# Second mixer's projections on unscaled rows, with the norm's factor applied behind each product

## The chip, the cores and the metric

The kernel is one program on one core of a Trainium2 chip. The metric is the device time of one execution in microseconds (us). The kernel before took 769.43 us (median of 3 runs, 769.27 to 769.75).

## The reference

Two transformer blocks run one after the other on 256 tokens of 1024 features, in float32.

```python
def reference(...):
    x = first_block(x, c, norm_mix_g, ...)      # adaLN, forgetting attention + pooling, 32-expert MoE, final rmsnorm
    return second_block(x, norm1_g_2, w_in_2, ...)

def hybrid_layer(x, ...):                        # the second block's mixer and feed-forward
    xn = rmsnorm_2(x, norm1_g[layer])
    u = xn @ w_in[layer]
    q_sb, k_sb, v_sb, f_raw, i_hg, q_hg, g_hg, gate_sb, gate_hg = jnp.split(u, list(c), axis=-1)
    o_sb = stick_breaking_attention(q_sb, k_sb, v_sb)
    f = lb + (1.0 - lb) * sigmoid(f_raw)
    o_hg = hgrn2_chunkwise(silu(q_hg), (1.0 - lb) * sigmoid(-f_raw), i_hg, log(f))
    o_hg = rmsnorm_2(o_hg, hg_norm_g) * silu(g_hg)
    g_a, g_b = sigmoid(gate_sb + bg[:D_MODEL]), sigmoid(gate_hg + bg[D_MODEL:])
    merged = g_a * (o_sb @ w_o_sb) + g_b * (o_hg @ w_o_hg)
    h = x + merged @ w_out
    a = square(relu(rmsnorm_2(h, norm2_g) @ w_ff1))
    return h + a @ w_ff2
```

The first block ends in an rmsnorm and the second begins with one. The kernel folds both into one factor for each token, which it calls `rq`. A factor for each token commutes with a product over the features, so it can be applied to the rows before `xn @ w_in` or to the result behind it.

## The kernel before

Every dense product is made of three passes of TensorE, because each operand is split in a high half and a low remainder of type fp32r: high times high, high times low, low times high (`mm3`). The weights come from HBM in pieces of 1 MB (128x2048 floats), loaded by SyncE (SP) into a ring of buffers in a fixed order. ScalarE (ACT) writes the high half of a piece (`whi`, L495, `act_pieces`), VectorE (DVE) then writes the remainder (`wlo`, L512, `dve_pieces`); a ring buffer is free for its next load when the remainder is written. There are four buffers of either half. The activations are split in the same way in `XH` and `XL`.

There is no planner: the order of work on each engine is written out by hand, one function for each engine, and semaphores join them. The pieces of the second mixer begin with piece 132 (`E1`): `f` uses pieces 132 and 133, `q2` 134 and 135, `g2` 136 and 137, `i2` 138 and 139, `sq` 140 and 141, `sk` 142 and 143, `sv` 144 and 145, then four pairs for the gates. `act_pieces(e, 137)` means: make high halves up to piece 136.

What stands around the change:

- The last expert group of the MoE (`pe_down`, `pe_combine`): the experts' results are made in two column halves n = 0 and 1. DVE scales a half to `ym` (L1331), TensorE adds it to the four accumulators of the residual rows (token half t, column half n).
- Then the norm. DVE multiplies the accumulators by a gain into `xn2` (`xg`, L1962). ACT and DVE sum squares (L1906, L1755, L2128), two tiny activations make `rq` (L1762, L1764), and DVE writes a diagonal matrix `hon` with `rq` on it (L1974, `factor`).
- Meanwhile TensorE runs four matmuls whose result nobody reads (`pe_awake`), then turns the 256 rows of 1024 features into 8 chunks of features by tokens (`n3`), by a matmul of `xn2` with `hon`, so that the turned rows come out scaled. ACT and DVE split each chunk (L1769, L1979), and between them the first pieces of weights. TensorE then computes `f`.
- DVE keeps the first block's output (`x_kept`, L1987), then prepares the lower bounds `lb` from a small table that SP loads after the MoE's end (L1989 to L2001). ACT takes the exponential of it (L1778) ahead of the high halves of pieces 134 to 136.
- Behind each product one engine reads the PSUM bank: DVE for `f` (L2006), ACT for `q2`, `g2` (silu, L1912), `sq`, `sk` (L737, L1819), `i2`, `sv` (L742) and the 16 gate chunks with their bias (`act_gate`, L1941).
- GpSimd (POOL) makes decay exponents for the four recurrent heads, ACT takes their exponential (`act_decays`), DVE multiplies (`dve_decays`), TensorE makes scores (`pe_head`) between the projections.
- The eight heads of the stick-breaking attention follow in a software pipeline over i = 1 to 10: scores `z`, softplus on ACT and DVE, weights `w`, their exponential on ACT (`w_exp`, L1839), product with the values (`sbv`). The last gate projections and the output projection of the recurrent heads (`o_hg`) stand between them. `act_sigmoids` at i = 2 and i = 5 loads the sigmoid's table, runs one activation over eight gate chunks (L1949) and loads the former table again.

SP has a queue of its own for loads, and POOL does no step that is moved here.

## Time and profile before

| | |
|---|---|
| median of 3 runs | 769.43 us |
| span of the profiled execution, first to last instruction | 767.3 us |
| what lies around the span (769.43 - 767.3) | 2.1 us |
| TensorE busy | 689.3 us, 90% |
| VectorE, ScalarE, GpSimd busy | 47%, 38%, 6% |
| end of the MoE to the start of the second mixer's products | 350 to 365 us of the span |
| second mixer | 365 to 583 us, then the feed-forward |

All times of places in the text are us from the start of the span. The profile names an instruction by its line, engine and operation, with the tile that it writes and what it reads. "PE" is TensorE's matmuls, "PEld" its weight loads. An fp32 matmul is recorded as two instructions. A bracket behind a row says how long the engine had been idle before it and what ended that. "PEclk" is the clock granted to TensorE, as a share of full speed.

### The profile page before, as it was taken

The numbers are of one execution on the slowest core, as the hardware profiler recorded it, in microseconds if no ns is written. First come the engines' busy times: TensorE is split into PE (matmuls) and PEld (weight loads), VectorE is DVE, ScalarE is ACT, GpSimd is POOL, SyncE is SP. The second block draws the span as 40 slices with busy tenths as digits, with TensorE's granted clock in tenths as the row PEclk, the third lists the DMA queues.
The fourth block names the chain that finished last, engine by engine and source line by source line (L and its number), as shares of the span: only waits on it lengthen the run. The fifth ranks groups of instructions, "written<-read, shape, count | busy, mean of one in ns | idle before, by whom it ended". The sixth has DMA issues, their size and how long they took to land.

```text
span 767.3 us, 13033 instructions
## 1 busy us (share of the span) xinstructions
PE 689.3 (90%) x5466; PEld 536.6 (70%) x5466; DVE 357.3 (47%) x569; ACT 295.3 (38%) x432; POOL 46.5 (6%) x84
## 2 busy tenths in 40 slices
PE   3999999899758677778999999999999999999996
PEld 2987778743323222223999989998979999999995
DVE  3568861521110000105846786536576744555443
ACT  4244530331111010005764553678355643354432
POOL 0000000000000000000074650000000000000000
PEclk9999999999988888879999999999999999999999
DMA  8999899999999999999855334414345445654001
GB/s 355 403 416 402 323 424 419 422 423 422 423 423 422 423 421 425 396 414 422 305 204 218 114 114 167 161 34 187 111 164 193 150 179 220 220 209 170 6 1 55
DMA packets 33038, 210.27 MB, mean 274 GB/s; under 512 B 4688, under 2 KB 5072, under 8 KB 8656
## 3 DMA queue, kind: packets, MB, share of 16 engines
q1 hardware_dynamic: 32976, 209.38, 68.4%
q8 instruction: 46, 0.75, 0.4%
q14 instruction: 16, 0.13, 0.0%
HBM read 208.32 MB, written 1.05 MB: 273 GB/s over the span
## 4 chain that ended last, share of the span: by engine, by line
PE 69%; DMA 20%; DVE 5%; ACT 3%; issue 2%; SPq 2%; DVEq 0%; ACTq 0%
PE psum L419 67%; DMA raw<-in_w_exp 16%; DMA raw<-in_w_in_t 3%; SPq L474 1%; PE psum L427 1%; DVE wlo L512 1%; ACT whi L495 1%; DMA raw<-in_w_ada_q 1%; DVE XL L1979 0%; DVE X L2428 0%; DVE acc L534 0%; ACT G L1283 0%; ACT XT L2375 0%; ACT Sp L838 0%; DVE ym L1331 0%
## 5 line engine op out<-in xcount | busy, mean ns | idle before, releaser
L419 PE MATMUL psum<-XH,whi 128*128 128x256 f32 x736 | 210.1, 286 | 4.3 <-DVE XL L665 3.2
L419 PE MATMUL psum<-XH,wlo 128*128 128x256 f32 x736 | 208.1, 283 | 0.0
L419 PE MATMUL psum<-XL,whi 128*128 128x256 f32 x736 | 207.9, 282 | 0.0
L512 DVE TENSOR_TENSOR wlo<-raw,whi 128x2048 fp32r<-128x2048 f32 (+1 forms) x88 | 169.0, 1958 | 48.9 <-ACT whi L495 48.9
L495 ACT ACTIVATE whi<-raw 128x2048 fp32r<-128x2048 f32 (+1 forms) x79 | 139.4, 1801 | 39.8 <-PE psum L419 22.4
L419 PEld LDWEIGHTS psum<-XH,whi 128*128 128x128 f32 x736 | 139.1, 189 | 7.9 <-DVE XL L665 3.6
L419 PEld LDWEIGHTS psum<-XL,whi 128*128 128x128 f32 x736 | 138.6, 188 | 0.3
L419 PEld LDWEIGHTS psum<-XH,wlo 128*128 128x128 f32 x736 | 138.8, 189 | 0.0
L419 PE MATMUL psum<-raw,G 128*32 128x512 f32 x456 | 69.3, 698 | 18.7 <-DMA raw<-in_w_exp 18.1
L419 PEld LDWEIGHTS psum<-raw,G 128*32 128x32 f32 x456 | 18.1, 125 | 57.1 <-issue 56.4
L419 PE MATMUL psum<-raw,XT 128*32 128x512 f32 x248 | 37.9, 747 | 19.3 <-DMA raw<-in_w_exp 18.1
L1267 ACT ACTIVATE WT<-psum 128x256 f32<-128x256 f32 x8 | 3.1, 384 | 134.7 <-PE psum L419 98.7
L419 PE MATMUL psum<-whi,FL 128*128 128x512 f32 (+1 forms) x132 | 50.6, 384 | 0.0
L419 PE MATMUL psum<-wlo,FH 128*128 128x512 f32 (+1 forms) x132 | 50.6, 384 | 0.0
L419 PE MATMUL psum<-whi,FH 128*128 128x512 f32 (+1 forms) x132 | 50.5, 383 | 0.0
L419 PEld LDWEIGHTS psum<-raw,XT 128*32 128x32 f32 x248 | 10.3, 132 | 42.1 <-issue 42.1
L1331 DVE TENSOR_TENSOR ym<-psum,GT 128x512 f32<-128x512 f32 x16 | 11.1, 691 | 58.7 <-PE psum L419 58.7
L1321 DVE TENSOR_TENSOR XT<-XT,psum 128x256 f32<-128x256 f32 x8 | 3.4, 421 | 67.0 <-ACT XT L1272 67.0
L1733 POOL TENSOR_TENSOR XT<-xn 128x128 f32<-128x128 f32 x12 | 9.3, 777 | 401.5 <-DVE xn L2018 388.2
L419 PE MATMUL psum<-ym,WT 128*128 128x512 f32 x64 | 29.1, 595 | 1.8 <-DVE ym L1331 1.8
L2395 DVE TENSOR_TENSOR af<-af,psum 128x512 f32<-128x512 f32 x16 | 11.0, 687 | 39.1 <-ACT af L2354 39.1
L2354 ACT ACTIVATE af<-psum 128x512 f32<-128x512 f32 x16 | 9.6, 599 | 50.4 <-PE psum L419 50.4
(347 smaller groups left out, 943.7 us busy)
## 6 DMA issues: line engine op xcount, KB each, us to landing
raw<-in_w_exp SPq DMA_DIRECT2D x85, 1024.0 KB, 22.7
raw<-in_w_ff SPq DMA_DIRECT2D x32, 1024.0 KB, 5.9
raw<-in_w_in SPq DMA_DIRECT2D x22, 1024.0 KB, 6.3
raw<-in_w_ada SPq DMA_DIRECT2D x16, 1024.0 KB, 11.7
raw<-in_w_in_t SPq DMA_DIRECT2D x8, 1024.0 KB, 18.0
X<-in_w_exp SPq DMA_DIRECT2D x5, 1024.0 KB, 24.8
raw<-in_w_ada_q SPq DMA_DIRECT2D x4, 1024.0 KB, 17.2
raw<-in_w_out_t SPq DMA_DIRECT2D x4, 1024.0 KB, 9.8
```

Source lines behind the costliest of these rows:

```text
L419: return e.matmul(o, l, r, start=start, stop=stop, skip_group_check=True)
L427: return e.transpose(o, x, C["ident"][0:p, 0:p])
L474: e.dma_start(dst, src).then_inc(small[name], 16)
L495: e.activation(whi[j % NS][:, x], ring[slot[i]][:, x], ACT.Copy).then_inc(*hi_made(("hi", j), ("hi", j, x.start // 1024)))
L512: e.tensor_tensor(wlo[j % NS][:, x], ring[slot[i]][:, x], whi[j % NS][:, x], ALU.subtract).then_inc(*steps_(("lo", j, x.start // 1024), *[ ...
L1267: e.activation(WT[y % 2][:, :], bank(("w", y))[:, 0:256], ACT.Copy).then_inc(*moe_act(("read", ("w", y)), ("WT", y)))
L1321: e.tensor_tensor(ac[b], sa[b], bank(("gu", y))[:, 256:512], ALU.mult).then_inc(*moe_dve(("read", ("gu", y)), ("act", y)))
L1331: e.tensor_tensor(ym[:, y % 2, cs], bank(("d", y, n))[:, :], GTF[:, cs], ALU.mult).then_inc(*moe_dve(("read", ("d", y, n)), ("y", y, n)))
L1733: e.tensor_tensor(ev[:, :, 1, :], bv[:, :, 1, :], ref, ALU.subtract).then_inc(*hyb_pool())
L2354: e.activation(af[q][:, :], bank((("ff1", j), q))[:, :], ACT.Relu).then_inc(*ff_act(("relu", j, q)))
L2395: e.tensor_tensor(af[q][:, :], af[q][:, :], bank((("ff1", j), q))[:, :], ALU.mult).then_inc(*ff_dve(("read", (("ff1", j), q)), ("square", ...
```

## The change

The turned rows are no longer scaled: `pe_n3` turns `xn2` by transposes against the identity. The first two groups of chunks (features 0 to 511) are turned between the experts' last `pe_down` and the last `pe_combine`, the other two between parts of `f`. The four `pe_awake` matmuls go. `rq` is computed later, and a new matmul with ones makes `rq` as a row in every partition (`rq_row`), which DVE copies to `RQ`. Every feature-major product is then multiplied by `RQ` by DVE as it leaves PSUM (`dve_scaled`, `dve_gate`), so ACT's readers of `sq`, `sk` and the gates go, and silu works on the scaled copy. The token-major products `i2` and `sv` take `rq` as ACT's scale. The gates' bias moves into the sigmoid, which becomes eight activations of one chunk in place of one over eight.

```diff
@@ -1505,6 +1506,9 @@
                     for n in range(2):
                         pe_down(e, db, y - 1, n)
                         if y == NQ:
+                            if n:
+                                pe_n3(e, Banks([1]), 0)
+                                pe_n3(e, Banks([3]), 1)
                             pe_combine(e, y - 1, n)
...
@@ -1750,27 +1754,24 @@
...
-            for t in range(2):
-                e.wait_ge(*at(("xg", t, 0)))
-                e.activation(flat(gates[:, 0:4, :])[:, 512 * t:512 * t + 512], xn2[:, t, 0:512], ACT.Square,
-                             accum_out=sq2[:, t:t + 1]).then_inc(*hyb_act(("sq2", t)))
-            high_part(e, E1, 0)
-            for t in range(2):
-                e.wait_ge(*at(("xg", t, 1)))
-                act_square(e, t, 1)
+            for q in range(4):
+                if q == 2:
+                    for t in range(2):
+                        act_square(e, t, 1)
+                high_part(e, E1 + q // 2, q % 2)
+                e.wait_ge(*at(("n3", "turned", q)))
+                for c in (2 * q, 2 * q + 1):
+                    e.activation(XH[:, c, :], bank(("n3", q))[:, 256 * (c % 2):256 * (c % 2) + 256], ACT.Copy,
+                                 scale=gcol[:, 2, c:c + 1]).then_inc(*hyb_act(("n3", "H", c)))
+            cur["act"] = E1 + 2
+            for t in range(2):
+                e.activation(flat(gates[:, 4 * t:4 * t + 4, :]), xn2[:, t, :], ACT.Square, accum_out=sq2[:, t:t + 1]).then_inc(
+                    *hyb_act(("sq2", t)))
...
-            high_part(e, E1, 1)
-            for q in range(4):
-                e.wait_ge(*at(("n3", "turned", q)))
-                for c in (2 * q, 2 * q + 1):
-                    e.activation(XH[:, c, :], bank(("n3", q))[:, 256 * (c % 2):256 * (c % 2) + 256], ACT.Copy,
-                                 scale=gcol[:, 2, c:c + 1]).then_inc(*hyb_act(("n3", "H", c)))
-                if q < 2:
-                    high_part(e, E1 + 1, q)
-            cur["act"] = E1 + 2
+            e.wait_ge(*at("s1"))
...
@@ -1798,30 +1799,23 @@
                 e.activation(hgb[:, h, :], tmpB[:, o:o + 256], ACT.Ln, bias=lb[:, h:h + 1], scale=oml[:, h:h + 1]).then_inc(
                     *hyb_act(("f_log", h)))
             e.preload_act_table(ACT.Silu)
+            act_pieces(e, 140)
             act_silu(e, hgq, "q2")
-            act_pieces(e, 140)
+            act_pieces(e, 142)
             act_silu(e, hgg, "g2")
             e.preload_act_table_set("natural_log_exp_and_others")
-            act_pieces(e, 142)
             act_decays(e, 0)
             for t in range(2):
-                act_rows(e, hgv, t, hyb_act, "i2")
+                act_rows(e, hgv, t, hyb_act, "i2", rq[:, t:t + 1])
             act_pieces(e, 144)
             for hd in range(4):
                 if hd == 0:
-                    act_copy(e, sbq, 0.125, hyb_act, "sq")
                     act_pieces(e, 146)
                 if hd < 3:
                     act_decays(e, hd + 1)
                 for q in range(2):
-                    if hd == 0:
-                        e.wait_ge(*at(("sk", "mm", q)))
-                        e.activation(flat(sbk[:, 2 * q:2 * q + 2, :]), bank(("sk", q))[:, :], ACT.Copy).then_inc(
-                            *hyb_act(("read", ("sk", q)), ("sk", "out", q)))
-                    elif hd == 1:
-                        act_rows(e, sbv, q, hyb_act, "sv")
-                    else:
-                        act_gate(e, 4 * (hd - 2), q)
+                    if hd == 1:
+                        act_rows(e, sbv, q, hyb_act, "sv", rq[:, q:q + 1])
                     if q == 0:
                         act_head(e, hd)
...
@@ -1838,8 +1832,6 @@
                         e.wait_ge(*at(("sbv", h - 2)))
                     e.activation(zs[h % 2], bank(("z", h))[:, 0:384], ACT.Exp).then_inc(*hyb_act(("read", ("z", h)), ("w_exp", h)))
                 act_pieces(e, SB_PIECES[i])
-                if 1 <= i <= 4:
-                    act_gate(e, 8 if i < 3 else 12, (i - 1) % 2)
...
         def act_square(e, t, n):
-            e.wait_ge(*at(("combined", NQ - 1, n, t)))
+            e.wait_ge(*at(("xg", t, n)))
             e.activation(flat((hgq, hgg)[t][:, 2 * n:2 * n + 2, :]), ps[4 + 2 * t + n][:, :], ACT.Square,
-                         accum_out=(ss, ss2)[n][:, t:t + 1]).then_inc(*hyb_act(("sq", t, n)))
+                         accum_out=(ss, ss2)[n][:, t:t + 1]).then_inc(*hyb_act(("sq", t, n), *[("read", ("acc", t))] if n else []))
 
         def act_silu(e, dst, name):
             for q in range(2):
-                e.wait_ge(*at((name, "mm", q)))
-                e.activation(flat(dst[:, 2 * q:2 * q + 2, :]), bank((name, q))[:, :], ACT.Silu).then_inc(
-                    *hyb_act(("read", (name, q)), (name, "out", q)))
+                e.wait_ge(*at((name, "scaled", q)))
+                e.activation(flat(dst[:, 2 * q:2 * q + 2, :]), flat(dst[:, 2 * q:2 * q + 2, :]), ACT.Silu).then_inc(
+                    *hyb_act((name, "out", q)))
...
-        def act_gate(e, base, q):
...
-                e.activation(gates[:, base + n, :], bank(("gate", base, q))[:, o:o + 256], ACT.Identity,
-                             bias=nbg[:, base + n:base + n + 1]).then_inc(
-                    *hyb_act(*[("read", ("gate", base, q))] if n % 2 else []))
-
         def act_sigmoids(e, o):
             e.preload_act_table(ACT.Sigmoid)
-            e.wait_ge(*hyb_act.last())
-            g = flat(gates[:, o:o + 8, :])
-            e.activation(g, g, ACT.Sigmoid).then_inc(*hyb_act(("sig", o)))
+            e.wait_ge(*loaded("bg"))
+            for n in range(o, o + 8):
+                e.wait_ge(*at(("gate", 4 * (n // 4), n % 4 // 2)))
+                e.activation(gates[:, n, :], gates[:, n, :], ACT.Sigmoid, bias=nbg[:, n:n + 1]).then_inc(*hyb_act(("sig", o)))
             e.preload_act_table_set("natural_log_exp_and_others")
...
         def dve_hybrid(e):
             e.wait_ge(*loaded("fin"))
-            for t, n in ((0, 0), (1, 0), (0, 1), (1, 1)):
-                cs = slice(512 * n, 512 * n + 512)
-                if t < n:
-                    dve_results(e, NQ - 1, (1,))
-                e.wait_ge(*at(("combined", NQ - 1, n, t) if n else ("sq", t, n)))
-                e.tensor_tensor(xn2[:, t, cs], ps[4 + 2 * t + n][:, :], GTM[:, cs], ALU.mult).then_inc(*hyb_dve(("xg", t, n)))
-            dve_second_sum(e, 0)
+            for t in range(2):
+                dve_xg(e, t, 0)
+            dve_results(e, NQ - 1, (1,))
+            low_part(e, E1, lo_dve, 0)
+            dve_n3(e, 0)
+            for t in range(2):
+                dve_xg(e, t, 1)
+            low_part(e, E1, lo_dve, 1)
+            dve_n3(e, 1)
+            dve_n3(e, 2)
+            low_part(e, E1 + 1, lo_dve, 0)
+            dve_n3(e, 3)
+            low_part(e, E1 + 1, lo_dve, 1)
+            cur["dve"] = E1 + 2
             e.wait_ge(*at(("sq", 1, 1)))
-            e.tensor_tensor(ss[:, :], ss[:, :], ss2[:, :], ALU.add).then_inc(*hyb_dve("s1", ("read", ("acc", 0)), ("read", ("acc", 1))))
-            dve_second_sum(e, 1)
-            e.wait_ge(*at("s1"))
+            e.tensor_tensor(ss[:, :], ss[:, :], ss2[:, :], ALU.add).then_inc(*hyb_dve("s1"))
+            e.wait_ge(*hyb_dve.last())
+            e.wait_ge(*at(("sq2", 1)))
             e.scalar_tensor_tensor(out=sq2[:, :], in0=ss[:, :], scalar=1e-6, in1=sq2[:, :], op0=ALU.mult, op1=ALU.add).then_inc(*hyb_dve())
             e.wait_ge(*hyb_dve.last())
-            e.scalar_tensor_tensor(out=rq[:, :], in0=sq2[:, :], scalar=D * 1e-12, in1=sq3[:, :], op0=ALU.add, op1=ALU.add).then_inc(
-                *hyb_dve("u"))
+            e.tensor_scalar(rq[:, :], sq2[:, :], D * 1e-12, None, ALU.add).then_inc(*hyb_dve("u"))
             e.wait_ge(*at("rq"))
             for t in range(2):
                 e.tensor_scalar(hon[:, t, :], C["ident"], rq[:, t:t + 1], None, ALU.mult).then_inc(*hyb_dve(("factor", t)))
-            low_part(e, E1, lo_dve, 0)
-            for q in range(4):
-                for c in (2 * q, 2 * q + 1):
-                    e.wait_ge(*at(("n3", "H", 2 * q + 1)))
-                    e.scalar_tensor_tensor(out=XL[:, c, :], in0=bank(("n3", q))[:, 256 * (c % 2):256 * (c % 2) + 256],
-                                           scalar=gcol[:, 2, c:c + 1], in1=XH[:, c, :], op0=ALU.mult, op1=ALU.subtract).then_inc(
-                        *hyb_dve(*[("n3", "ready", q), ("read", ("n3", q))] if c % 2 else []))
-                if q < 3:
-                    low_part(e, E1 + (q + 1) // 2, lo_dve, (q + 1) % 2)
-            cur["dve"] = E1 + 2
...
+            e.wait_ge(*at("rq_row"))
+            e.tensor_copy(RQ, bank("rq_row")[:, 0:256]).then_inc(*hyb_dve(("read", "rq_row")))
+            e.wait_ge(*hyb_dve.last())
             for q in range(2):
-                e.wait_ge(*at(("f", "mm", q)))
-                e.tensor_scalar(tmpA[:, 512 * q:512 * q + 512], bank(("f", q))[:, :], -1.0, 87.0, ALU.mult, ALU.min).then_inc(
-                    *hyb_dve(("read", ("f", q)), ("f_neg", q)))
+                dve_scaled(e, tmpA.rearrange("p (a b) -> p a b", a=4), q, "f", -1.0)
+                e.wait_ge(*hyb_dve.last())
+                e.tensor_scalar(tmpA[:, 512 * q:512 * q + 512], tmpA[:, 512 * q:512 * q + 512], 87.0, None, ALU.min).then_inc(
+                    *hyb_dve(("f_neg", q)))
...
+            dve_pieces(e, 140)
+            for q in range(2):
+                dve_scaled(e, hgq, q, "q2")
             dve_pieces(e, 142)
+            for q in range(2):
+                dve_scaled(e, hgg, q, "g2")
             dve_decays(e, 0)
             dve_pieces(e, 144)
             for hd in range(4):
                 if hd == 0:
+                    for q in range(2):
+                        dve_scaled(e, sbq, q, "sq", 0.125)
                     dve_head(e, 0)
                     dve_pieces(e, 146)
                 if hd < 3:
                     dve_decays(e, hd + 1)
+                if hd == 0:
+                    dve_scaled(e, sbk, 0, "sk")
+                if hd >= 2:
+                    dve_gate(e, 4 * (hd - 2), 0)
...
+                if hd == 0:
+                    dve_scaled(e, sbk, 1, "sk")
+                if hd == 2:
+                    dve_gate(e, 0, 1)
...
                 dve_pieces(e, 148 + 2 * hd)
+                if hd == 3:
+                    dve_gate(e, 4, 1)
...
+                if i <= 4:
+                    dve_gate(e, 8 if i < 3 else 12, (i - 1) % 2)
...
-        def dve_second_sum(e, t):
-            e.wait_ge(*at(("xg", t, 1)))
-            e.scalar_tensor_tensor(out=flat(gates[:, 4:8, :])[:, 512 * t:512 * t + 512], in0=xn2[:, t, 512:1024], scalar=1.0,
...
+        def dve_xg(e, t, n):
+            cs = slice(512 * n, 512 * n + 512)
+            e.wait_ge(*at(("combined", NQ - 1, n, t)))
+            e.tensor_tensor(xn2[:, t, cs], ps[4 + 2 * t + n][:, :], GTM[:, cs], ALU.mult).then_inc(*hyb_dve(("xg", t, n)))
...
+        def dve_scaled(e, dst, q, name, by=None):
+
+            d, p = dst[:, 2 * q:2 * q + 2, :], bank((name, q))[:, :].rearrange("p (a b) -> p a b", a=2)
+            e.wait_ge(*at((name, "mm", q)))
+            if by is None:
+                i = e.tensor_tensor(d, p, row2(RQ), ALU.mult)
+            else:
+                i = e.scalar_tensor_tensor(out=d, in0=p, scalar=by, in1=row2(RQ), op0=ALU.mult, op1=ALU.mult)
+            i.then_inc(*hyb_dve(("read", (name, q)), (name, "scaled", q)))
+
+        def dve_gate(e, base, q):
+            if base == 8:
+                e.wait_ge(*at(("hm_last", 3)))
+            e.wait_ge(*at(("gate", base, "mm", q)))
+            e.tensor_tensor(gates[:, base + 2 * q:base + 2 * q + 2, :], bank(("gate", base, q))[:, :].rearrange("p (a b) -> p a b", a=2),
+                            row2(RQ), ALU.mult).then_inc(*hyb_dve(("read", ("gate", base, q)), ("gate", base, q)))
...
-            pe_awake(e, 4, ("gu", NQ - 1))
-            for q in range(4):
-                p = banks.take(e, ("n3", q))
-                for c in (2 * q, 2 * q + 1):
-                    for t in range(2):
-                        e.wait_ge(*at(("factor", t)))
-                        i = mm(e, p[:, 256 * (c % 2) + 128 * t:256 * (c % 2) + 128 * t + 128], xn2[:, t, 128 * c:128 * c + 128],
-                               hon[:, t, :], c % 2 + t == 0, True)
-                i.then_inc(*hyb_pe(("n3", "turned", q)))
-            for q in range(4):
-                feature_part(e, banks, w2(q // 2), (2 * q, 2 * q + 1), "f", "n3", hyb_pe)
+            fb = Banks([0, 2])
+            feature_part(e, fb, w2(0), (0, 1), "f", "n3", hyb_pe)
+            pe_n3(e, Banks([4]), 2)
+            pe_n3(e, Banks([5]), 3)
+            feature_part(e, fb, w2(0), (2, 3), "f", "n3", hyb_pe)
+            feature_part(e, fb, w2(1), (4, 5), "f", "n3", hyb_pe)
+            p = Banks([3]).take(e, "rq_row")
+            for t in range(2):
+                e.wait_ge(*at(("factor", t)))
+                i = mm(e, p[:, 128 * t:128 * t + 128], C["ones"], hon[:, t, :], t == 0, True)
+            i.then_inc(*hyb_pe("rq_row"))
+            feature_part(e, fb, w2(1), (6, 7), "f", "n3", hyb_pe)
...
+        def pe_n3(e, banks, q):
+            p = banks.take(e, ("n3", q))
+            for t in range(2):
+                e.wait_ge(*at(("xg", t, q // 2)))
+                for c in (2 * q, 2 * q + 1):
+                    i = turn(e, p[:, 256 * (c % 2) + 128 * t:256 * (c % 2) + 128 * t + 128], xn2[:, t, 128 * c:128 * c + 128])
+            i.then_inc(*hyb_pe(("n3", "turned", q)))
```

## Rows read from the trace of the kernel before

**Rows 1.** Page: busy time by engine, and the chain that ended last by engine

```profile
PE 689.3 (90%) x5466; PEld 536.6 (70%) x5466; DVE 357.3 (47%) x569; ACT 295.3 (38%) x432; POOL 46.5 (6%) x84
PE 69%; DMA 20%; DVE 5%; ACT 3%; issue 2%; SPq 2%; DVEq 0%; ACTq 0%
```

**Rows 2.** Chain of waits in order of time, 355 to 577 (start, us, what)

```profile
355.50 5.39 PE psum L419 x12
...
371.33 1.91 ACT whi L495
...
373.34 1.76 DVE wlo L512
...
375.55 2.30 DVE wlo L512
...
575.58 0.87 PE psum L427 x8
```

**Rows 3.** Timeline of TensorE, 355 to 378 (start, us, engine, line, operation, tiles, count, idle before)

```profile
355.50 1.96 PE L419 MATMUL psum<-ym,WT 128*128 128x512 f32 x4 [0.91 <-DVE ym L1331]
360.92 3.81 PE L419 MATMUL psum<-hon,xn 128*128 128x128 f32 x32
364.48 0.37 PE L419 MATMUL psum<-XH,whi 128*128 128x256 f32 x1
...
377.98 0.36 PE L419 MATMUL psum<-XH,whi 128*128 128x256 f32 x1 [0.43 <-DVE wlo L512]
```

**Rows 4.** Timeline of ACT and DVE, 352 to 379

```profile
354.67 0.69 DVE L1331 TENSOR_TENSOR ym<-psum,GT 128x512 f32<-128x512 f32 x1 [0.47 <-PE psum L419]
363.75 1.21 DVE L512 TENSOR_TENSOR wlo<-raw,whi 128x1024 fp32r<-128x1024 f32 x1
370.83 0.15 DVE L1989 TENSOR_TENSOR lb<-lbr 128x4 f32<-128x4 f32 x1
371.22 0.20 ACT L1778 ACTIVATE lb<-lb 128x4 f32<-128x4 f32 x1 [3.79 <-DVE lb L1991]
377.75 1.28 DVE L2006 TENSOR_SCALAR xn<-psum 128x512 f32<-128x512 f32 x2
```

**Rows 5.** SP's issue at 357 to 359, and that load's time to landing (last column)

```profile
357.75 0.33 SPq L474 DMA_DIRECT2D lbr<-in_lb_cols  x1
lbr<-in_lb_cols SPq DMA_DIRECT2D x1, 4.0 KB, 11.8
```

**Rows 6.** Timeline of ACT, DVE and PE, 519 to 535

```profile
519.98 0.84 ACT L1941 ACTIVATE gates<-psum,nbg 128x256 f32<-128x256 f32 x2 [2.08 <-PE psum L419]
520.71 1.05 ACT L1847 ACTIVATE XH<-hgg 128x1024 fp32r<-128x1024 f32 x1
523.80 3.70 ACT L495 ACTIVATE whi<-raw 128x2048 fp32r<-128x2048 f32 x2
528.82 1.92 ACT L1949 ACTIVATE gates<-gates 128x2048 f32<-128x2048 f32 x1
534.13 0.85 PE L419 MATMUL psum<-sbv,xn 128*128 128x64 f32 x6 [1.31 <-issue]
```

**Rows 7.** ACT by line: duration ns min/median/max, first and last start, forms

```profile
L1941 ACT ACTIVATE gates<-psum,nbg x16: 467/471/477, 462.2 to 520.3; 128x256 f32<-128x256 f32 x16
L1798 ACT ACTIVATE hgb<-xn,lb,oml x4: 583/588/590, 383.5 to 385.0; 128x256 f32<-128x256 f32 x4
```

**Rows 8.** TensorE's two idle stretches nearest in length (timeline), and the clock behind one (stretch, us, PE busy, PEclk, DMA)

```profile
18.46 0.39 PE L419 MATMUL psum<-XH,whi 128*128 128x256 f32 x1 [2.38 <-DVE XL L665]
201.07 5.34 PE L419 MATMUL psum<-raw,G 128*32 128x512 f32 x32 [3.36 <-DMA raw<-in_w_exp]
201.50:204.25 2.75, 2.75 (x17) 0.50 1.01 429
```

**Rows 9.** The core from 378 to 486: us, busy of PE, PEld, DVE, ACT, POOL, PEclk, DMA, GB/s

```profile
378.00:486.00 108.00, 108.00 (x1200) 99.66 (x1201) 73.19 (x125) 59.16 (x79) 46.36 (x80) 1.00 0.47 174
```

**Rows 10.** Timeline of DVE, 435 to 439, ahead of the second head's scores

```profile
438.91 0.49 DVE L2147 TENSOR_TENSOR xn<-psum,cst 128x320 f32<-128x320 f32 x1 [2.82 <-PE psum L419]
```

More of the change, by code:

```diff
@@ L738, in act_copy, with act_rows @@
                     *steps_(("read", (name, q)), (name, "out", q)))
-        def act_rows(e, dst, t, steps_, name):
+        def act_rows(e, dst, t, steps_, name, scale=1.0):
             e.wait_ge(*at((name, "mm", t)))
-            e.activation(dst[:, t, :], bank((name, t))[:, :], ACT.Copy).then_inc(*steps_(("read", (name, t)), (name, "out", t)))
+            e.activation(dst[:, t, :], bank((name, t))[:, :], ACT.Copy, scale=scale).then_inc(*steps_(("read", (name, t)), (name, "out", t)))
         def sp_mixer(e):
@@ L2277, in pe_z @@
                 for q in range(2):
-                    e.wait_ge(*at(("sq", "out", q)))
-                    e.wait_ge(*at(("sk", "out", q)))
+                    e.wait_ge(*at(("sq", "scaled", q)))
+                    e.wait_ge(*at(("sk", "scaled", q)))
             mm(e, p[:, 0:256], sbk[r, h // 2, 0:128], sbq[r, h // 2, 0:256], True, False)
@@ L2488, in tensor_engine @@
             pe_moe(e, Banks(list(range(8))))
-            banks = Banks(list(range(8)))
+            banks = Banks([6, 7, 0, 1, 2, 3, 4, 5])
             pe_hybrid(e, banks)
```

16 lines of the change are left out of this document (7 added, 9 removed).

## The prediction, on record before the changed kernel ran

> **What bounds the kernel now.** I read the page first. TensorE is busy 90% of the span and the chain that ended last is 69% TensorE [rows 1], so only time in which TensorE waits, or does work that can go, is worth anything. The chain in order of time shows where that is: beside the MoE's loads, which the change leaves alone, it leaves TensorE around the end of the MoE and is back on it at 378 [rows 2]. The timeline of TensorE there has three things to see [rows 3]: the last combine at 355.50, then matmuls that only keep the engine busy, then the scaled turning at 360.92 (32 records, 3.81 us) and `f` at 364.48. One wait follows, 0.43 us at 377.98 for a weight remainder. Behind it TensorE is busy for all of the next 108 us [rows 9], so whatever is saved must be saved before 378 and kept.
>
> **What sets 377.98.** This is the step on which the forecast rests. `q2` needs the remainders of pieces 134 and 135. DVE makes them at 373.34 and 375.55, behind ACT's high half of 134 at 371.33 [rows 2]. ACT could start that only behind its tiny exponential of `lb` (371.22), which waits for DVE's two `lb` steps from 370.83 [rows 4]. From the first `lb` step to the high half is 0.50 us, from the high half to TensorE's restart 6.65 us. So `f` may begin much earlier and still gain only what this ACT and DVE chain gains.
>
> **The front, step by step.** Removed on TensorE: four matmuls that nobody reads (in the 5.39 us of [rows 2]) and 16 scaling matmuls, 3.81 us. Added: 16 transposes; eight of the same kind took 0.87 us for the feed-forward's norm [rows 2]. Eight of them fall between the last `pe_down` and the combine, where TensorE idles 0.91 us for DVE's `ym` [rows 3]: they fit, and I take them as free. DVE's `xg` of the first half no longer waits for ACT's square, so ACT's square, high half and first split of `XH` follow from about 352.7. By the durations of the rows (half of 1.91 for half a high piece [rows 2], 1.21 for half a remainder, 0.69 for a PSUM product of 512 [rows 4]) the first `XL` is ready at 357.4, right behind the combine's end (355.50 + 1.96). `f` starts at 357.5 instead of 364.48. Its 96 matmuls took from 364.48 to about 375.8, 11.4 us; with 0.9 us of turning and about 1.0 us of waiting for and making `rq_row` in between it ends at 370.8.
>
> ACT and DVE meanwhile alternate through the eight chunk splits and four half pieces, ACT squares 2 x 1024 columns for `rq` (about 1.2 us each), and DVE has `factor` at 367.3 and `x_kept` at 368.6. That is 2.2 us ahead of 370.83. But `lb` reads a table that SP issues at 357.75, when the MoE has ended, and which lands 11.8 us later, at 369.55 [rows 5]; it stands behind the pieces in the queue, and nothing here moves it. Before, that load was hidden by 1.3 us; now it is what comes last. `lb` starts at 369.6, the high half of 134 at 370.1, and TensorE gets the remainder of 135 at 370.1 + 6.65 = 376.75: **a gain of 1.2 us**, against 7 us for the start of `f`.
>
> **What the gap does to TensorE.** Between `f`'s end at 370.8 and the first remainder (370.1 + 375.55 - 371.33 = 374.3) TensorE is now idle 3.5 us. The trace of before has an idle stretch of 2.38 us behind which TensorE kept its clock (18.46), and one of 3.36 us behind which it ran at the granted clock 0.50, which is 1.2 GHz, through 204.25 at least [rows 8]. I take the nearer row: the clock falls. The 12 matmuls that need piece 134 alone (1.4 us at full clock) then take 2.8, from 374.4 to 377.2, of which 0.45 lies behind piece 135; if the low stretch is as long as that row's, 3.2 us, its last 0.4 loses 0.2 more. Together 0.7 us, bounds 0 (no fall) and 1.6 (3.2 us halved with no cover). Front in all: -1.2 + 0.7 = **-0.5 us**. The Trainium skill speaks against the change here: "TensorE: Matmul & The Clock Gate", section "What's actually happening", says that throttled is the default state and activity releases it, and its Part 4 that transposes do not count as activity in the same way. By that rule the fall is likely and the front gives 0.5; without it the front would give 1.2. The row at 201.07 agrees for an idle engine, and no row here tests transposes.
>
> **DVE's new work.** Sixteen products of 512 columns from PSUM at 0.69 [rows 4], 11 us in all, move to DVE or are new; `f` needs a second instruction of about 0.4 for each half and DVE copies `RQ` (0.4). Queued behind a product that waits for its projection are DVE's next remainders, decays and heads. For `f` this adds 1.5 us on DVE behind 376.7, so the scan and POOL's decays come about 0.3 us later than before; their users are 10 us away. The tightest place is the second head: the product of `sk`'s second half ends 0.7 us behind `sk`'s end, and DVE was idle 2.82 us before it read the scores at 438.91 [rows 10]. It fits. At the end of the recurrent heads ACT's gate copy goes (0.84 less before two high halves) and a DVE product comes (0.69): -0.1. I take all others at 0; if one has no cover it costs its 0.69, bounds 0 to 3.
>
> **The second sigmoid.** At i = 5 the order on ACT sets TensorE: high halves at 523.80, table, sigmoid over 2048 columns at 528.82 (1.92), table, `z`, `w_exp`, and TensorE, idle 1.31 us, starts `sbv` at 534.13 [rows 6]. The change takes one gate copy out ahead of `XH` (0.73 between the starts 519.98 and 520.71), and makes the sigmoid eight activations of 256 columns with a bias pointer. No such row exists from SBUF. From below: the gate copies, a bias pointer from PSUM, 0.84 for two, so 0.37 from start to start; from above: L1798, two pointers from SBUF, four from 383.5 to 385.0, so 0.50 [rows 7]. I take 0.40, near the lower row, since there is one pointer: 8 x 0.40 + 0.1 = 3.3 against 1.92, +1.4 (bounds +1.1 and +2.2). The 0.73 is not given back: `w_exp` of i = 5 waits for DVE's mask, and DVE now has `XL` and then a 0.69 gate product before it, so ACT's high halves start only 0.1 earlier. **+1.3 us** at 534.13, with TensorE idle until then. The earlier `XH` only makes TensorE arrive sooner (it waited 0.5 there). The first sigmoid at i = 2 has TensorE busy over it and costs 0. The Trainium skill ("ScalarE: Activation LUTs", section "What ACT_TABLE_LOAD costs") gives 186 ns plus 0.833 a column, about 93 more for each pointer and 93 of overlap; by it one of these is 0.49 long and 0.40 apart, an estimate, and 2048 columns take 1.89 where this trace has 1.92.
>
> **Sum.** -0.5 - 0.1 + 1.3 = +0.7 us. The profiled execution's span is 767.3, with 2.1 around it that do not change: 767.3 + 0.7 + 2.1 = 770.1, against the median 769.43. What a measurement of this kernel can tell from no change is 0.2%, 1.5 us.
>
> **The rivals.**
> A. The forecast: one fall of the clock, at 374; the sigmoid's chain at 534. 770.1, its own range 769.6 to 770.9. Chance 0.40.
> B. The clock holds in the gap at 371. For it: the row at 18.46, which kept it behind 2.38 us; against it: the gap is longer than the 3.36 that lost it. -1.2 - 0.1 + 1.3 = 0.0: 769.4. Chance 0.15.
> C. Slower: the clock also falls at 534. TensorE arrives 0.5 sooner and is released 1.3 later, so its wait is 1.31 + 0.5 + 1.3 = 3.1 us, between the row that kept the clock and the row that lost it; it decides if the clock falls in that wait. Half clock on the products behind costs 1.4 (bounds 0.7 and 1.6), all exposed. +0.7 + 1.4 = +2.1: 771.5. Chance 0.22.
> D. Slower by DVE: a remainder or a head's operands queue behind a product that waits for TensorE, in two or three places that I took as covered. Against it the idle times of DVE (47% busy). +3: 772.4. Chance 0.08.
> E. Faster: the table lands before 368.6 because the queue is drained earlier, or the front's chain otherwise ends at 2.2 us, and the clock holds; the eight sigmoids overlap fully (+0.6). -2.2 - 0.1 + 0.5 = -1.8: 767.6. For it: DVE is ready at 368.6. Against it: the landing is counted from an issue that does not move. Chance 0.15.
>
> **The numbers.** Slower by over 0.2% (above 771.0): C and D nearly whole and the edge of A, 0.33. Faster (below 767.9): most of E, 0.12. Within: 0.55. The range 768.3 to 772.2 leaves out E's core and part of D, under 2 in 10.
>
> **What would show it.** Right: `f` starts near 357.5; `lb` at 369.6 behind its load, with DVE idle before it; TensorE idle some 3.5 us ahead of `q2`, PEclk 0.5 behind it; `sbv` at 534 released by `w_exp` with an idle time of about 3 us; the sum of the eight sigmoids 3.3 us. Wrong: `lb` not waiting; `q2` running at full clock; a new wait of TensorE for `scaled`, `gate` or `qk` in the middle; or `f` starting later than 359, which would close the gap and with it the fall of the clock.

## The result: 4.3 us slower

The changed kernel's median is 773.6 us against 769.35 us for the kernel before, run beside it; the ratio is 1.0053, 95% interval 1.0041 to 1.0065. A second session gave 1.0050 (1.0037 to 1.0062). The forecast was 770.1 with a range up to 772.2: wrong, and on the side of rival C, but twice as far. The profiled execution took 774.81 us (span 773.0). In it even the last combine starts 1.7 us later than before, at 357.20 against 355.50. In the other profiles of kernels with the changed front it starts at 355.4 to 357.3, in those with the old front at 355.5 to 356.0, so that part is scatter of the MoE (the means lie 0.3 us apart). The combine of the other column half, ahead of the first changed instruction of TensorE, is just as late already: 350.79 before and 352.49 here, each 4.71 us ahead of the last one. All comparisons below are made from that combine on.

The page's first lines and the chain by engine, which answer to [rows 1]:

```profile
PE 689.9 (89%) x5446; PEld 540.0 (70%) x5446; DVE 367.3 (48%) x584; ACT 291.3 (38%) x426; POOL 45.5 (6%) x84
PE 67%; DMA 22%; DVE 4%; ACT 3%; issue 2%; SPq 1%; DVEq 0%; ACTq 0%
```

TensorE has 20 records fewer and yet 0.6 us more busy time: some matmuls have become longer. The front, TensorE's timeline (answers to [rows 3]; the 32 scaling matmuls are gone):

```profile
352.49 1.95 PE L420 MATMUL psum<-ym,WT 128*128 128x512 f32 x4 [0.90 <-DVE ym L1332]
...
356.23 1.09 PE L428 MATMUL psum<-cst,xn 128*128 128x128 f32 x8
357.20 1.96 PE L420 MATMUL psum<-ym,WT 128*128 128x512 f32 x4
359.81 0.36 PE L420 MATMUL psum<-XH,whi 128*128 128x256 f32 x1 [0.65 <-DVE XL L2133]
376.76 0.55 PE L420 MATMUL psum<-XH,whi 128*128 128x256 f32 x1 [3.61 <-DVE wlo L513]
```

`f` begins 2.6 us behind the combine's start instead of 9.0, and then TensorE waits 3.61 us ahead of `q2` (forecast 3.5). The chain of waits names what holds it (answers to [rows 2]), and the issue and landing of the table stand below it (to [rows 5]):

```profile
359.45 12.34 DMA lbr<-in_lb_cols
...
371.81 0.17 DVE lb L1965
...
372.32 1.91 ACT whi L496
...
374.32 2.30 DVE wlo L513
...
376.76 23.34 PE psum L420 x183
```

```profile
lbr<-in_lb_cols SPq DMA_DIRECT2D x1, 4.0 KB, 12.3
```

The second sigmoid, ACT's and TensorE's timelines (to [rows 6]), and the eight activations by line (to [rows 7]):

```profile
525.42 3.70 ACT L496 ACTIVATE whi<-raw 128x2048 fp32r<-128x2048 f32 x2
530.44 3.30 ACT L1929 ACTIVATE gates<-gates,nbg 128x256 f32<-128x256 f32 x8
536.56 0.47 ACT L1833 ACTIVATE xn<-psum 128x384 f32<-128x384 f32 x1
537.13 1.51 PE L420 MATMUL psum<-sbv,xn 128*128 128x64 f32 x6 [3.27 <-issue]
```

```profile
L1929 ACT ACTIVATE gates<-gates,nbg x16: 492/494/512, 500.9 to 533.2; 128x256 f32<-128x256 f32 x16
```

The third line is `w_exp`, and `sbv` starts at its end. Here and below, "`sbv` of i = 5" is the product that the sigmoid at i = 5 holds up; in TensorE's own loop it stands at i = 7 (head 5).

What follows each of the two waits, and what lies between (windows: stretch, us, busy of PE, PEld, DVE, ACT, POOL, then PEclk, the granted clock; to [rows 8, 9]):

```profile
377.00:378.00 1.00, 1.00 (x6) 1.00 (x7) 1.00 (x1) 0.82 (x1) 0.00 (x0) 0.50 0.77 106
380.00:488.00 108.00, 108.00 (x1202) 99.67 (x1201) 80.24 (x137) 55.17 (x69) 45.32 (x80) 1.00 0.46 170
537.00:540.00 3.00, 2.87 (x13) 2.90 (x14) 2.47 (x7) 1.68 (x6) 0.00 (x0) 0.50 0.03 14
540.00:543.00 3.00, 3.00 (x16) 3.00 (x15) 1.33 (x1) 1.64 (x1) 0.00 (x0) 0.50 0.00 0
```

The granted clock is 0.50, which is 1.2 GHz, for 3.4 us around `q2`'s start (376.5 to 379.9), and for 6.8 us (536.9 to 543.7) around the start of `sbv` of i = 5. `sbv` itself is the sign: six matmuls take 1.51 us, where before they took 0.85.

**Where the time went.** Three marks divide the rest of the program: the start of `z` of head 3 (494.94 before, 496.56 changed), that of `sbv` of i = 5, and the first turning of the feed-forward's norm (575 and 581). The distances, in us, with the wait ahead of `sbv` and how long the clock was low around it:

| profile | combine to `z` | `z` to `sbv` | wait | clock low | `sbv` to turning |
|---|---|---|---|---|---|
| before | 139.44 | 39.19 | 1.31 | none | 41.28 |
| changed | 139.36 | 40.57 | 3.27 | 6.8 | 44.27 |
| changed, again (e4) | 140.39 | 40.49 | 3.27 | 6.8 | 44.07 |
| e1 bias on DVE | 139.89 | 39.76 | 2.54 | none | 41.29 |
| e2 six matmuls in the wait | 139.16 | 40.45 | 0.63 | none | 41.30 |
| e3 before, 8 sigmoids | 139.96 | 39.83 | 1.96 | none | 41.30 |
| e5 sigmoid 12 and 4 | 139.84 | 38.90 | 1.67 | none | 41.31 |
| e6 table earlier | 138.43 | 40.51 | 3.31 | 3.4 | 43.30 |
| e7 pieces ahead of table | 135.72 | 40.50 | 3.27 | 3.4 | 42.81 |
| e8 e7 and e5 | 135.89 | 38.90 | 1.68 | none | 41.37 |
| e9 matmuls behind a wrong wait | 145.84 | 40.57 | 3.30 | 6.8 | 44.21 |
| e10 before, biased sigmoids | 139.45 | 40.38 | 2.74 | 3.4 | 42.82 |
| e11 sigmoid 9 and 7 | 139.04 | 40.10 | 2.87 | 3.4 | 42.83 |
| e12 e8, X later | 136.91 | 38.97 | 1.70 | none | 41.29 |
| e13 matmuls ahead of `q2` | 138.69 | 40.50 | 3.31 | 3.4 | 42.82 |
| e14 two matmuls in the wait | 140.63 | 40.45 | 2.37 | 3.4 | 42.83 |

Changed against before: -0.1, +1.4, +3.0, together +4.3 us.

### The profile page after: what moved, and what is told of

Its sections match the earlier page's. It is cut to its first block, busy times and chain, and to the rows that moved or that the text cites. A ratio compares the mean times of both kernels' runs of the same rounds, so it can differ in the third digit from the quotient of the medians.

```text
span 773.0 us, 12998 instructions
## 1 busy us (share of the span) xinstructions
PE 689.9 (89%) x5446; PEld 540.0 (70%) x5446; DVE 367.3 (48%) x584; ACT 291.3 (38%) x426; POOL 45.5 (6%) x84
## 4 chain that ended last, share of the span: by engine, by line
PE 67%; DMA 22%; DVE 4%; ACT 3%; issue 2%; SPq 1%; DVEq 0%; ACTq 0%
PE psum L420 65%; DMA raw<-in_w_exp 17%; DMA raw<-in_w_in_t 3%; DMA lbr<-in_lb_cols 2%; PE psum L428 1%; SPq L475 1%; ACT whi L496 1%; DMA raw<-in_w_ada_q 1%; DVE wlo L513 1%; ACT gates L1929 0%; DVE X L2460 0%; DVE acc L535 0%; ACT XT L2407 0%; ACT Sp L839 0%; DVE gates L2082 0%
## 5 line engine op out<-in xcount | busy, mean ns | idle before, releaser
L420 PEld LDWEIGHTS psum<-XH,whi 128*128 128x128 f32 x736 | 140.8, 191 | 11.6 <-issue 7.8
L420 PEld LDWEIGHTS psum<-XL,whi 128*128 128x128 f32 x736 | 140.4, 191 | 0.3
L420 PEld LDWEIGHTS psum<-XH,wlo 128*128 128x128 f32 x736 | 140.5, 191 | 0.0
L420 PE MATMUL psum<-raw,G 128*32 128x512 f32 x456 | 67.5, 674 | 19.2 <-DMA raw<-in_w_exp 19.2
L420 PEld LDWEIGHTS psum<-raw,XT 128*32 128x32 f32 x248 | 10.3, 132 | 43.3 <-issue 43.3
## 6 DMA issues: line engine op xcount, KB each, us to landing
raw<-in_w_ada SPq DMA_DIRECT2D x16, 1024.0 KB, 11.8
raw<-in_w_in_t SPq DMA_DIRECT2D x8, 1024.0 KB, 18.5
```

The costliest lines, as they stand in the source:

```text
L420: return e.matmul(o, l, r, start=start, stop=stop, skip_group_check=True)
```

## The experiments

All were timed beside the kernel before, in 4 to 12 executions each; one execution of each is profiled. The diffs are shortened; in them lines of the changed kernel (or, for e3 and e10, of the kernel before) begin with a minus.

**e1: the bias on DVE, one sigmoid again.**

```
+ (dve_gate, base >= 8)  e.tensor_scalar(gates[:, n, :], gates[:, n, :], nbg[:, n:n + 1], None, ALU.add)
- e.activation(gates[:, n, :], gates[:, n, :], ACT.Sigmoid, bias=nbg[:, n:n + 1])   # 8 of them
+ e.activation(g, g, ACT.Sigmoid)   # 2048 columns
```

> The changed kernel, but for the second set of gates (chunks 8 to 15) DVE adds the bias behind its product (eight instructions of 256 columns more on DVE), and the sigmoid is one activation of 2048 columns again, as before. Theory (the loss sits at the second sigmoid: 1.3 us of longer sigmoid and then about 3.0 us because TensorE's clock falls behind a 3.27 us wait): the wait ahead of sbv of i = 5 goes from 3.27 back to some 1.8 us, the granted clock behind it stays 1.00, and the kernel is 4 us faster than the changed one, within 0.2% of the kernel before (ratio 0.998 to 1.001). Rival 1 (only the activations' own 1.3 us are lost there, the rest of the loss is upstream, at the MoE's end, or is scatter): about 772.5, ratio 1.004. Rival 2 (DVE's added products are what costs): DVE has yet more to do here, so no gain or a loss: ratio 1.006 or more.

Measured 1.0033 (1.0022 to 1.0044): by the ratios 1.3 us faster than the changed kernel (2.0 by the medians) and not the 4 expected. Its profiled execution, the fastest of eight (770.1 to 774.5), kept its clock behind the wait:

```profile
535.07 0.85 PE L420 MATMUL psum<-sbv,xn 128*128 128x64 f32 x6 [2.54 <-issue]
```

The wait is 2.54, not 1.8: DVE's bias steps delay its mask, and ACT's high halves with it (from `z` to `sbv` 0.57 more than before). So it took half of the chain away. Its combine starts at 355.42, the earliest of all profiles, which is part of why this execution is fast. Whether the slower executions lost the clock isn't seen, since one only is profiled. The expectation missed: by time alone rival 1 (ratio 1.004) fits, and e1 can't exclude it. e2 does.

**e2: work in the wait.**

```
  p, vs, z = banks.take(e, ("sbv", h)), ...
+ for _ in range(6 if i == 7 else 0):
+     mm(e, p[:, 256:512], C["ident"], cst[:, NCONST - 256:], True, True)
```

> The changed kernel with six matmuls of 256 columns that nobody reads (about 0.45 us each by the 3.60 us of four of 512 columns, together 2.7 us), put into TensorE's wait of 3.27 us ahead of sbv of i = 5. Nothing else changes. Theory: sbv still starts at the same place (w_exp releases it), the granted clock behind it is 1.00 instead of 0.50 for 6.7 us, and 3.0 us come back: about 770.6 to 771.5, ratio 1.002. Rival (the clock does not depend on this wait, or the low stretch costs nothing): no change, ratio 1.005.

Measured 1.0021 (1.0012 to 1.0030), 2.5 us below e4 by the medians, about what the theory said. `sbv` comes as late as in the changed kernel, but at full clock:

```profile
532.37 2.76 PE L420 MATMUL psum<-cst 128*128 128x256 f32 x12
535.76 0.88 PE L420 MATMUL psum<-sbv,xn 128*128 128x64 f32 x6 [0.63 <-ACT xn L1833]
```

This shows the last column's 2.8 to 3.0 us to be the clock's price: work that nobody reads gives it back.

**e3: the kernel before with its sigmoid in eight.**

```
- e.activation(g, g, ACT.Sigmoid)
+ for n in range(8): e.activation(g[:, 256 * n:256 * n + 256], ..., ACT.Sigmoid)   # o == 8 only
```

> The kernel before, with one edit: its second sigmoid over 2048 columns is cut into eight activations of 256 columns, without a bias. All else is as before. Theory: the sigmoid takes about 1.3 us longer (3.2 instead of 1.92), TensorE's wait ahead of sbv of i = 5 grows from 1.31 to about 2.6 us; if that is long enough the clock falls behind it and costs up to 3.0 more. So +1.3 us (clock holds, 770.7, ratio 1.0017) to +4.3 us (clock falls, 773.7, ratio 1.0056). Rival (the sigmoid's chain is hidden elsewhere): no change.

Measured 1.0009 (1.0000 to 1.0018), half of the least that was expected, because the eight take 2.57 us and not 3.2. One such activation takes 0.40 us without a bias pointer, so they start 0.31 apart; with a pointer (L1929 above, 0.49 each) they start 0.40 apart:

```profile
529.69 2.57 ACT L1951 ACTIVATE gates<-gates 128x256 f32<-128x256 f32 x8
535.65 0.85 PE L419 MATMUL psum<-sbv,xn 128*128 128x64 f32 x6 [1.96 <-issue]
```

`sbv` moved by 0.64; 2.57 - 1.92 is 0.65. The chain is not hidden, but half of its growth is the bias pointer's.

**e4: the changed kernel again.**

> The changed kernel as it is, timed again beside the others. Theory: 772 to 775, and the clock behind the wait at sbv of i = 5 is low again. Rival for the 1.7 us by which the profiled execution was late already at the MoE's end: if that belongs to the change, it is there in this profile too and absent from the profiles of the kernel before; if it is scatter of the execution, kernels with the same front differ in it as well.

773.99, ratio 1.0050. The combine starts at 356.05 here: of the 1.7 us of the first profile 1.15 were not there again. The clock falls at the same two places.

**e5: the same sigmoids, shared out 12 and 4.**

```
- if i in (2, 5): act_sigmoids(e, 0 if i == 2 else 8)
+ if i in (3, 5): act_sigmoids(e, *((0, 12) if i == 3 else (12, 4)))
```

> The changed kernel, with the sixteen chunks of the gates' sigmoid shared out otherwise: 12 of them at i = 3 and 4 at i = 5, instead of 8 at i = 2 and 8 at i = 5. The work is the same. Theory: four activations fewer at i = 5 are 4 x 0.41 = 1.65 us; the wait of 3.27 us ahead of sbv becomes 1.6, the clock stays at 1.00, so 1.65 + 2.7 = 4.3 us faster than the changed kernel (ratio to before about 0.9995). It would fail if the twelve at i = 3 (4.9 us and two tables) are not covered by TensorE's gate matmuls there: then a new wait of TensorE at i = 4 or 5. Rival (DVE's mask or the products are what releases w_exp): no more than e1 gave.

Measured 0.9998 (0.9989 to 1.0007), 769.4: by the ratios 4.0 us come back, where 4.3 were expected.

```profile
534.28 0.85 PE L420 MATMUL psum<-sbv,xn 128*128 128x64 f32 x6 [1.67 <-issue]
```

```profile
535.00:538.00 3.00, 3.00 (x27) 3.00 (x26) 1.65 (x5) 1.71 (x3) 0.00 (x0) 1.00 0.18 74
```

Everything else of the change is in this kernel: the new front, the products on DVE, the row. Together they cost nothing that can be measured, and bring nothing; the 0.3 us by which `sbv` is sooner here than in the kernel before is this edit's own.

**e6: the table loaded near the program's start.**

```
+ lbr = sb("lbr", [128, 2, 4])                 # a place of its own
- (sp_hybrid)  sp_small(e, "lb", lbr[:, :, :], a["lb_cols"])
+ (sp, behind sp_load(e, 16))  the same line
```

> The changed kernel with the 4 KB table lb_cols in a place of its own in SBUF, loaded near the start of the program instead of behind the MoE's end, where it landed 12.3 us after its issue. Theory (the landing releases DVE's lb, and through it ACT's high half of piece 134): DVE's lb starts right behind x_kept, 0.8 us sooner (1.9 in the profile of e4), TensorE's idle time ahead of q2 falls from 3.6 to about 2.8 us; then the clock may hold there too, another 0.7. So 0.8 to 1.9 us faster than the changed kernel, ratio 1.002 to 1.004. Rival (the piece's order on ACT and DVE alone sets q2): no change.

No gain in the median: 1.0056 (1.0043 to 1.0068). In the profile the step did what it should:

```profile
367.83 1.42 DVE L1963 TENSOR_SCALAR X<-xn,rs 128x1024 f32<-128x1024 f32 x2
369.16 0.15 DVE L1965 TENSOR_TENSOR lb<-lbr 128x4 f32<-128x4 f32 x1
374.11 0.36 PE L420 MATMUL psum<-XH,whi 128*128 128x256 f32 x1 [2.74 <-DVE wlo L513]
```

```profile
375.00:378.00 3.00, 3.00 (x16) 3.00 (x16) 2.93 (x5) 0.44 (x2) 0.00 (x0) 0.50 0.88 328
```

`q2` starts 18.5 us behind the combine instead of 19.2 to 20.3, so the landing did hold it; but a wait of 2.74 lost the clock as well. A gain of 0.9 us lies within both intervals; the timing can't tell the theory's lower end from the rival's none.

**e7: the pieces ahead of the table's steps.**

```
- (ACT) wait lb_less; Exp(lb); act_pieces(e, 137)
+ (ACT) act_pieces(e, 137); wait lb_less; Exp(lb)
- (DVE) lb steps; dve_pieces(e, 136)
+ (DVE) dve_pieces(e, 136); wait for the table; lb steps
```

> The changed kernel with two moves in the front: ACT makes the high halves of pieces 134 to 136 ahead of its exponential of lb, and DVE the remainders of 134 and 135 ahead of its steps on lb. The load of the table stays late. Theory: the first remainder is ready at about 373.6 on the scale of the changed kernel's profile instead of 376.6, TensorE goes from f (ends 373.2) to q2 with under 1 us of idle time, the clock stays at 1.00: 2.7 to 3.2 + 0.7 us faster than the changed kernel, ratio about 1.001. Rival (behind q2 TensorE only meets the next late piece, so the gain is given back before the heads): the idle time shows again within 20 us of q2, and less than 1 us is left.

Measured 0.9993 (0.9982 to 1.0005), by the ratios 4.4 us faster than the changed kernel. The order, not the load, was what mattered:

```profile
372.09 0.36 PE L420 MATMUL psum<-XH,whi 128*128 128x256 f32 x1 [0.78 <-DVE wlo L513]
...
531.78 0.85 PE L420 MATMUL psum<-sbv,xn 128*128 128x64 f32 x6 [3.27 <-issue]
```

```profile
374.00:377.00 3.00, 2.71 (x23) 2.73 (x24) 2.49 (x12) 0.21 (x1) 0.00 (x0) 1.00 0.99 412
534.00:537.00 3.00, 3.00 (x16) 3.00 (x15) 0.84 (x2) 2.28 (x2) 0.00 (x0) 0.51 0.00 0
```

`z` is 4 us sooner than the 139.8 that is the mean of the seven profiles with the unmended front. The rival (given back at the next piece) falls. The wait at `sbv` is unmoved, and the clock falls there still, though in this profile for 3.4 us only.

**e8: e5 and e7 together.**

> The moves of e7 and the shares of e5 together. Theory: the two places are apart and their gains add: about 4.3 + 3.5 us off the changed kernel, 766, ratio to before 0.995. Rival (TensorE arriving earlier at i = 5 only waits longer there, since ACT and DVE set that place): the sum falls short by what the wait ahead of sbv grows, and the clock could fall again.

766.8, ratio 0.9962 (0.9949 to 0.9975): faster than both kernels. By the ratios e5's edit brings 2.4 us on top of e7 and 4.0 alone, though in the table the two columns add; the wait at `sbv` is 1.68, so the rival (TensorE only waits longer there) falls. In the profile of e7 the clock was low for only 3.4 us, which fits a smaller gain; with five executions the difference isn't settled.

**e9: matmuls ahead of `q2`, behind the wrong wait.**

> The changed kernel with eight matmuls of 256 columns that nobody reads (about 3.6 us together) between f and q2, where TensorE waits 3.6 us. Theory: the granted clock behind q2's start is 1.00 instead of 0.50 for 3.4 us; by the forecast's estimate this returns 0.7 us, while the second wait (0.5 us, for the remainder of 135) comes back; ratio 1.004. Rival (the low clock there costs what it cost at sbv, half of its 3.4 us): 1.5 us or more, ratio 1.003. Either way the clock at sbv of i = 5 still falls.

1.0115, where 1.003 to 1.004 was expected. The extra matmuls were made to wait for DVE's copy of the row, which is queued behind both remainders:

```profile
377.84 0.42 DVE L1981 COPY rqrow<-psum 128x256 f32<-128x256 f32 x1
378.31 5.50 PE L420 MATMUL psum<-cst 128*128 128x256 f32 x16 [6.12 <-DVE rqrow L1981]
```

It leaves the question of the clock's price at `q2` open, and shows what one wait on the wrong side of a queue costs.

**e10: one part of the change alone, in the kernel before.**

```
- act_gate:  ACT.Identity, bias=nbg[:, base + n:base + n + 1]     # base >= 8
+ act_gate:  ACT.Copy
- e.activation(g, g, ACT.Sigmoid)
+ for n in range(8, 16): e.activation(gates[:, n, :], ..., ACT.Sigmoid, bias=nbg[:, n:n + 1])
```

> The kernel before, with one part of the change alone: for the second set of gates ACT copies the projection without its bias, and the sigmoid is eight activations of 256 columns that add it. Theory: 3.30 us instead of 1.92 at i = 5, sbv 1.3 us later against z of head 3 (40.5 us between them, 39.2 in the kernel before), a wait of 2.6 to 2.7 us. If the clock holds, +1.3 us, ratio 1.0017; if it falls for 3.4 us, +2.9, 1.004; for 6.8 us, +4.2, 1.0055. A wait of 2.54 kept it in e1 and one of 2.74 lost it in e6, so some executions either way are likeliest: 1.002 to 1.004. Rival (only the eight's 0.65 of e3 counts, the rest is DVE's doing): 1.0009.

1.0027 (1.0015 to 1.0038), as expected: `sbv` 1.2 us later, the clock low from 536.2 to 539.6.

```profile
535.81 1.13 PE L419 MATMUL psum<-sbv,xn 128*128 128x64 f32 x6 [2.74 <-issue]
```

```profile
536.00:538.00 2.00, 2.00 (x12) 2.00 (x12) 2.00 (x6) 0.72 (x2) 0.00 (x0) 0.56 0.01 4
```

By the ratios this one part makes half of the whole slowdown, 1.2 us by the chain and 1.5 by the clock in the profile, in a kernel with nothing else of the change.

**e11: 9 and 7 sigmoids.** As e5, with `(0, 9)` and `(9, 7)`.

> As e5, but 9 chunks at i = 3 and 7 at i = 5. Theory: one activation fewer at i = 5 shortens the wait ahead of sbv by 0.41, to 2.86 us, which is still longer than the 2.74 behind which the clock fell in e6: only 0.4 us faster than the changed kernel, ratio 1.0045. Rival (what e5 gained came of the place of the first set, i = 3 instead of 2, not of the wait): near e5, ratio 1.000.

1.0035 (1.0023 to 1.0047). The place of the first set gains nothing; the number at i = 5 does. Wait 2.87, clock low for 3.4 us.

**e12: X's scalings behind the remainders too.**

> As e8 (pieces ahead of the table, sigmoids 12 and 4), and DVE's two scalings of X (1.42 us) also behind the remainders of 134 and 135. Theory: DVE can begin the first remainder when ACT has made half of its high part, 0.5 us sooner; TensorE's two waits at q2 (0.78 and 0.55) shrink by up to 0.5; ratio to before 0.9955 (e8: 0.9962). Rival (ACT's high parts set the place): no change against e8.

0.9956 (0.9942 to 0.9970), no different from e8. The theory falls and the rival holds: the waits at `q2` are those of e8 (0.78, 0.54), and DVE begins the first remainder 14.2 us behind the combine in both, having been idle for 1.81 us instead of 0.46. ACT's high half sets it.

**e13: e9 mended**, the matmuls in a bank long free, with no wait for the row.

> As e9, but the eight matmuls write into a bank that has long been free, so TensorE waits for nothing ahead of them. Theory: they fill the 3.6 us ahead of q2, the granted clock at q2 stays 1.00, and the wait for the second remainder (0.5 us) comes back; against the changed kernel z of head 3 starts 0.6 us sooner, ratio 1.0040 to 1.0045. Rival (a low stretch of 3.4 us costs 1.5 us here as it does at sbv): ratio 1.003.

1.0030 (1.0015 to 1.0045). The clock holds at `q2`, and the second remainder's wait is back:

```profile
372.92 3.62 PE L420 MATMUL psum<-cst 128*128 128x256 f32 x16
376.76 0.36 PE L420 MATMUL psum<-XH,whi 128*128 128x256 f32 x1 [0.22 <-DVE wlo L513]
378.96 0.36 PE L420 MATMUL psum<-XH,whi 128*128 128x256 f32 x1 [0.54 <-DVE wlo L513]
```

`z` is 1.1 us sooner than the mean of 139.8, between the theory's 0.6 and the rival's 1.5. The ratio is 1.5 us below the changed kernel's 1.0050, which is the rival's figure, with 1 us of uncertainty on each: not settled.

**e14: two matmuls instead of six ahead of `sbv`.**

> As e2, with two matmuls of 256 columns (0.9 us) instead of six, at the beginning of the wait ahead of sbv of i = 5. Idle time left in one piece: 3.27 - 0.9 = 2.4 us, less than the 2.54 behind which the clock held in e1. Theory (the length of the idle time decides): the clock holds and the kernel is as fast as e2, ratio 1.002. Rival (what counts is how much work is missing there): the clock falls as in the changed kernel, ratio 1.004 to 1.005.

1.0044 (1.0028 to 1.0061). My theory falls. Less idle time is left in one piece than in e1, and the clock falls all the same, 1.4 us after `sbv` has started:

```profile
537.21 0.88 PE L420 MATMUL psum<-sbv,xn 128*128 128x64 f32 x6 [2.37 <-ACT xn L1833]
```

```profile
538.00:541.00 3.00, 3.00 (x18) 3.00 (x18) 1.63 (x5) 1.71 (x3) 0.00 (x0) 0.60 0.00 0
```

## Why the prediction was wrong, step by step

**The start of `f`, the eight transposes under the last combine:** right. The combine isn't delayed, and `f` begins 2.6 us behind its start (forecast 2.0).

**The table as what comes last in the front:** right; the chain names it, and e6 takes it away. Its size was off. The load landed 12.0 to 13.1 us after its issue with the changed front, and 11.8, 12.7 and 13.6 in the three profiles with the old one, so the 11.8 of [rows 5] was the shortest of all. In e3, with the old front, DVE waited for it too:

```profile
371.70 0.16 DVE L1991 TENSOR_TENSOR lb<-lbr 128x4 f32<-128x4 f32 x1 [0.43 <-DMA lbr<-in_lb_cols]
```

So "hidden by 1.3 us" held for one profile only. The second remainder reaches TensorE 21.7 us behind the combine (e1, e5 and e13), against 22.5 before: 0.8 and not 1.2.

**The clock behind `q2`'s wait:** right that it falls; it did in every profile with the unfilled wait of 2.7 to 4.7 us. The forecast priced it at 0.7. By `z`, against the 138.7 of e13, where it held, it cost 0.4 to 1.7 in the six profiles with 3.4 us of low clock (139.0 to 140.4, in the mean 0.9) and 1.9 in e14 (6.8 us low); e13 is one profile, and e4's 1.7 has a later table in it. The front as a whole brought nothing: `z` stands at 139.8 as the mean of seven profiles (139.0 to 140.6) and at 139.6 as the mean of the three with the old front. The Trainium skill ("TensorE: Matmul & The Clock Gate", "What's actually happening") takes throttled as the default state, and the granted clock of 0.50 behind each such wait agrees; whether transposes count, no run here shows.

**DVE's products, taken as covered:** right. TensorE is busy for all of the 108 us behind 380, and e5 has them all and equals the kernel before.

**The second sigmoid:** right, and nearly exact. 0.40 apart was forecast and measured, 3.3 us for the eight was forecast and 3.30 measured, `sbv` later by 1.3 to 1.4. The wait there is 3.27 where 3.1 was forecast. The estimate from the Trainium skill ("ScalarE: Activation LUTs", "What ACT_TABLE_LOAD costs"), 0.49 long and 0.40 apart, agrees with the row too (492 to 512 ns).

**The step that failed** is "C. Slower: the clock also falls at 534", with a chance of 0.22 and a price of 1.4 (bounds 0.7 and 1.6); the sum of the forecast has nothing for it. A wait of 3.27 to 3.31 lost the clock in six profiles of six. I let the kept clock behind 2.38 us [rows 8] pull this chance down, though the forecast's own wait was nearer to the 3.36 that lost it, and I had taken the same row as decisive at `q2`. The price was sized by one low stretch of 3.2 us. The table shows two sizes: 3.4 us low costs 1.5 (2.0 in e6), 6.8 us costs 2.8 to 3.0. With that and the 0.6 missing from the front and the heads, -0.5 - 0.1 + 1.3 becomes 0 + 1.3 + 3.0 = 4.3, the result. With a low stretch of 3.4 us the same sum would be 2.8 (an estimate), 772.2.

Both sizes stood in the trace of before. Behind its start (10.3 us without a matmul, and the clock at 1.00) it has nine waits of 3.36 us or more, all in the MoE, and the clock fell at each: four low stretches of 3.4 us, four of 6.8 and one of 10.2. I had used the first (201.07) alone. One of the long ones, which runs from 290.0 to 296.9:

```profile
291.69 6.19 PE L419 MATMUL psum<-raw,G 128*32 128x512 f32 x32 [3.83 <-DMA raw<-in_w_exp]
290.50:296.50 6.00, 4.82 (x24) 0.50 1.01 427
```

What stays open: why the low stretch is sometimes one length and sometimes two. In e7 and in the changed kernel the same wait of 3.27 us was followed by either. The traces do sort them in part, by what TensorE did when the clock fell. Where it had already restarted, the low stretch was 3.4 us each time: four times in the MoE of before, four times at `q2`, six times at `sbv`. Where it was still idle, it was 6.8 at `sbv` (changed, e4, e9) and 6.8 or 10.2 in that MoE, yet at `q2` 3.4 three times (changed, e2, e4) and 6.8 twice (e9, e14). Which of the two a wait gets, no run here controls.

## What to carry to other kernels

A wait of the bounding engine that grows is to be priced twice: by its own growth, and by what the engine loses around it when its clock falls, which here was one to two times as much (1.5 to 3.0 us against 1.2 to 1.4). Before work is moved from one large instruction into many with a pointer each, look where that instruction stands: off the path it was free at i = 2, on it the same edit cost 2 us in e10 and 4 us in the changed kernel, with the clock. And a gain at the start of a chain (6.4 us for `f`) is worth only what the next dependence lets through: here a small table's steps stood ahead of two large pieces in the queues of ACT and DVE, and changing that order (e7) brought 4.4 us, while loading the table earlier did not measurably help.
